# Four rounded and two raw weight slots, and a new order of half-units around the norms

## The reference, cut to what matters

```
for i in range(2):
    a = nsa_mixer(x, ...) if i == 0 else moba_mixer(x, ...)     # ends with  out @ w_o
    x = layer_norm(ALPHA * x + a, ln1_g[i], ln1_b[i])
    f = (silu(x @ wg) * (x @ wu)) @ wd                          # D_FF = 2816
    x = layer_norm(ALPHA * x + f, ln2_g[i], ln2_b[i])
```

## Time and profile before

| | us |
|---|---|
| median of 3 runs | 690.97 |
| lowest, highest | 690.02, 695.6 |
| profiled execution, its own time | 695.23 |
| its span in the trace | 693.5 |

### The profile page before, as it was taken

The page is one execution under the profiler, slowest core; times in us unless marked ns, Lnnn a source line. Parts: engine busy times, 40 slices in busy tenths (PEclk is TensorE's granted clock), DMA queues, the critical chain, the costliest instruction groups (busy, mean ns, idle before and its releaser), DMA issues.

```text
span 693.5 us, 8675 instructions
## 1 busy us (share of the span) xinstructions
PE 653.0 (94%) x3274; PEld 520.2 (75%) x3274; DVE 405.6 (58%) x529; ACT 309.2 (45%) x434; POOL 21.9 (3%) x64
## 2 busy tenths in 40 slices
PE   5899989998899999999997999989799999999995
PEld 4697865567688888888875888757578888888883
DVE  3645488875855544444458565675865444454446
ACT  4624557754253333444433544683343333444430
POOL 2000000000100000000002000000200000000001
PEclk9999999999999999999999999999999999999998
DMA  8954150002665554555543745303356555555501
GB/s 299 415 218 182 62 183 1 2 10 112 194 232 181 181 181 181 184 188 193 195 154 134 266 169 180 157 1 122 121 190 235 181 181 185 185 190 195 198 14 60
DMA packets 18282, 112.97 MB, mean 163 GB/s; under 512 B 2768, under 2 KB 3024, under 8 KB 5584
## 3 DMA queue, kind: packets, MB, share of 16 engines
q1 hardware_dynamic: 16384, 103.18, 41.3%
q10 hardware_dynamic: 720, 5.24, 2.0%
q0 software_dynamic: 1152, 4.19, 1.7%
HBM read 111.56 MB, written 1.05 MB: 162 GB/s over the span
## 4 chain that ended last, share of the span: by engine, by line
PE 76%; DVE 13%; ACT 4%; issue 2%; POOL 2%; SPq 1%; DMA 1%; POOLq 0%; DVEq 0%
PE ps L963 23%; PE ps L965 22%; PE ps L964 22%; DVE w_lo L640 3%; ACT arena L512 2%; DVE neg_max L790 1%; PE ps L1220 1%; DVE bn L856 1%; DVE x L851 1%; PE ps L1137 1%; DVE x L874 1%; DMA raw<-stream 1%; DVE arena L807 1%; PE ps L1068 1%; POOL rstd L367 1%
## 5 line engine op out<-in xcount | busy, mean ns | idle before, releaser
L640 DVE TENSOR_TENSOR w_lo<-raw,w_hi 128x2048 fp32r<-128x2048 f32 (+1 forms) x98 | 220.1, 2248 | 137.9 <-ACT w_hi L385 137.7
L963 PE MATMUL ps<-w_hi,a_hi 128*128 128x512 f32 x592 | 238.5, 403 | 16.3 <-DVE w_lo L640 11.4
L964 PE MATMUL ps<-w_lo,a_hi 128*128 128x512 f32 x592 | 233.5, 394 | 0.0
L965 PE MATMUL ps<-w_hi,a_lo 128*128 128x512 f32 x592 | 233.3, 394 | 0.0
L385 ACT ACTIVATE w_hi<-raw 128x2048 fp32r<-128x2048 f32 (+1 forms) x98 | 184.0, 1877 | 110.1 <-PE ps L965 103.4
L963 PEld LDWEIGHTS ps<-w_hi,a_hi 128*128 128x128 f32 x592 | 113.0, 191 | 43.4 <-DVE w_lo L640 12.3
L965 PEld LDWEIGHTS ps<-w_hi,a_lo 128*128 128x128 f32 x592 | 112.8, 191 | 24.5
L964 PEld LDWEIGHTS ps<-w_lo,a_hi 128*128 128x128 f32 x592 | 112.8, 191 | 22.2
L963 PE MATMUL ps<-w_hi,h_hi 128*128 128x512 f32 x160 | 62.4, 390 | 0.0
L965 PE MATMUL ps<-w_hi,h_lo 128*128 128x512 f32 x160 | 62.3, 389 | 0.0
L964 PE MATMUL ps<-w_lo,h_hi 128*128 128x512 f32 x160 | 62.2, 389 | 0.0
(11 more groups left out here) (144 smaller groups left out, 499.8 us busy)
## 6 DMA issues: line engine op xcount, KB each, us to landing
raw<-stream SPq DMA_DIRECT2D x94, 1024.0 KB, 4.8
gain<-norms POOLq DMA_DIRECT2D x8, 512.0 KB, 5.0
arena<-w ACTq DMA_DIRECT2D x4, 1024.0 KB, 8.1
raw<-stream SPq DMA_DIRECT2D x4, 512.0 KB, 8.5
twice<-x_cols SPq DMA_DIRECT2D x4, 256.0 KB, 7.3
x<-x_rows ACTq DMA_DIRECT2D x1, 1024.0 KB, 4.9
out<-x SPq DMA_DIRECT2D x4, 256.0 KB, 2.1
wg_raw<-w_gates SPq DMA_DIRECT2D x1, 192.0 KB, 9.7
```

Source lines behind the costliest of these rows:

```text
L640: return nc.vector.tensor_tensor(dst, a, b, ALU.subtract)
L963: nc.tensor.matmul(dst, hi, m_hi, start=start, stop=False)
L964: nc.tensor.matmul(dst, hi, m_lo, start=False, stop=False)
L965: return nc.tensor.matmul(dst, lo, m_hi, start=False, stop=stop)
```

## The change

- `w_hi` and `w_lo` get four slots, `raw` gets two. A load now waits for the remainder of the unit two before; a rounding for TensorE to be done with the unit four before. ScalarE and VectorE take units one place earlier in most of the written order.
- Output projection: the half-units in the last two jobs are now of half 0, so that right after the last job the last two units complete the sums of half 0; then come the four half-units of half 1, with `turn_x` of half 0 between the second and the third. In `attend` ScalarE and VectorE make the fourth output unit inside the last job, where it was made after it.
- Norm: VectorE adds eps itself; GpSimd only does the power. VectorE makes `a_lo` of half 0 and two units' remainders before the first quarter of half 1, a third remainder before its last quarter.
- First chunk: between half 0 and half 1 TensorE does the first unit of the next chunk for half 0, half of its tiles before and half after `turn_x` of half 1. In norms 0 and 2 it first waits for `var_ready` of half 1, since the bank was still read. In the projection of layer 1 the second chunk then lacks that half-unit.
- Network: chunk 1 gets other PSUM banks and is written out on ScalarE and VectorE too; the loop over chunks 2 to 9 holds four chunks a pass on all three engines. `turn_x` for norm 1 goes ahead of the last 6 matmuls.
- Other places in which only an index, a bank or a bound of `round_to` or `rest_to` follows from this are left out below.

```diff
 UNIT = 2048
-SLOTS = 3
+RAW = 2
+SLOTS = 4
...
 
-        SUM_BANK = [0, 4, 0, 4]
+        CHUNK_BANKS = ((3, 1), (0, 3))
+
+        AT_ONCE = 4
+
+        SUM_BANK = [(2, 3, 0, 1), (4, 5, 6, 7)] * 2
+
+        TURN_BANK = [(4, 5, 6, 7), (0, 1, 4, 5)] * 2
...
-                    sp.wait_ge(lo_ready, (t - 1) * SLOTS + s + 1)
-                    unit = stream[bass.ds(t * SLOTS + s, 1), :, :].rearrange("a p n -> (a p) n")
+            with sp.Fori(1, UNITS // RAW) as t:
+                for s in range(RAW):
+
+                    sp.wait_ge(lo_ready, (t - 1) * RAW + s + 1)
+                    unit = stream[bass.ds(t * RAW + s, 1), :, :].rearrange("a p n -> (a p) n")
                     sp.dma_start(raw[:, s, :], unit).then_inc(raw_in[s], 16)
...
             def roots(l):
                 for half in range(HALF):
                     gp.wait_ge(var_ready, 2 * l + half + 1)
-                    link(nc.gpsimd.tensor_scalar(var_eps[:, l, half:half + 1], mean_var[:, l, half, 1:2],
-                                                 1.0, EPS, ALU.mult, ALU.add))
                     nc.gpsimd.tensor_tensor(rstd[:, l, half:half + 1], var_eps[:, l, half:half + 1],
...
-            def round_unit(s, arrived, used):
-                act.wait_ge(raw_in[s], arrived)
-                if used is not None:
-                    act.wait_ge(w_used, used)
-                copy(w_hi[:, s, :], raw[:, s, :]).then_inc(hi_ready, 1)
+            def round_unit(u, later=0):
+
+                act.wait_ge(raw_in[u % RAW], later * (16 // RAW) + 16 * (u // RAW + 1))
+                if u >= SLOTS:
+                    act.wait_ge(w_used, later + (u - SLOTS + 1))
+                copy(w_hi[:, u % SLOTS, :], raw[:, u % RAW, :]).then_inc(hi_ready, 1)
...
                         outputs_hi(i - 2)
-                    if i == jobs - 2:
-                        round_to(u + 3)
+                    if i >= jobs - 2:
+                        round_to(u + 3 + i - (jobs - 2))
...
-                nc.scalar.activation(silu[:, 0, :], ps[:, 0, 0:FC], ACT.Silu).then_inc(first_silu, 1)
+                silu_half(0, CHUNK_BANKS[0][0]).then_inc(first_silu, 1)
                 act.wait_ge(w_used, u0 + 2)
-                nc.scalar.activation(silu[:, 1, :], ps[:, 1, 0:FC], ACT.Silu).then_inc(silu_ready, 1)
-                round_to(u0 + 4)
+                silu_half(1, CHUNK_BANKS[0][1]).then_inc(silu_ready, 1)
+                round_to(u0 + 5)
                 hidden_hi(0)
-                round_to(u0 + 5)
-                with act.Fori(1, NFC - 1) as c:
-                    round_in(c, 2)
-                    silu_of(c, 3 * c + (u0 + 1))
-                    round_in(c, 3)
-                    hidden_hi(c)
-                    round_in(c, 4)
-                units[0] = u0 + 3 * (NFC - 1) + 2
+                round_to(u0 + 7)
+                act.wait_ge(w_used, u0 + 4)
+                silu_half(0, CHUNK_BANKS[1][0])
+                silu_half(1, CHUNK_BANKS[1][1]).then_inc(silu_ready, 1)
+                round_to(u0 + 8)
+                hidden_hi(1)
+                round_to(u0 + 9)
+                with act.Fori(0, (NFC - 3) // AT_ONCE) as t:
+                    for j in range(AT_ONCE):
+                        c, at = AT_ONCE * t + (2 + j), u0 + 3 * (2 + j)
+                        round_unit(at + 3, 3 * AT_ONCE * t)
+                        silu_of(c, 3 * AT_ONCE * t + (at + 1))
+                        round_unit(at + 4, 3 * AT_ONCE * t)
+                        hidden_hi(c)
+                        round_unit(at + 5, 3 * AT_ONCE * t)
+                units[0] = u0 + 3 * (NFC - 1) + 3
                 c = NFC - 1
-                round_to(u0 + 3 * c + 3)
+                round_to(min(UNITS, u0 + 3 * c + 4))
                 silu_of(c, u0 + 3 * c + 1)
                 hidden_hi(c, last_hi)
                 round_to(min(UNITS, u0 + 3 * c + 5))
...
 
                     dve.wait_ge(v_step, quarter_statistics(half, 1))
-                    nc.vector.bn_aggr(mean_var[:, l, half, :], bn[:, :, :].rearrange("p a b -> p (a b)")).then_inc(var_ready, 1)
-                    dve.wait_ge(var_ready, 2 * l + half + 1)
+                    aggregated = step(nc.vector.bn_aggr(mean_var[:, l, half, :], bn[:, :, :].rearrange("p a b -> p (a b)")))
+                    dve.wait_ge(v_step, aggregated)
+                    nc.vector.tensor_scalar(var_eps[:, l, half:half + 1], mean_var[:, l, half, 1:2],
+                                            EPS, None, ALU.add).then_inc(var_ready, 1)
 
...
                 finish(0)
                 if l < 3:
                     rest_to(u + 1)
-                quarter_statistics(1, 0)
-                if l < 3:
                     columns_lo(0, 0)
                     columns_lo(0, 1)
                     rest_to(u + 2)
+                quarter_statistics(1, 0)
+                if l < 3:
+                    rest_to(u + 3)
                 last_quarter_statistics(1)
                 finish(1)
...
-                with dve.Fori(1, NFC - 1) as c:
-                    rest_in(c, 2)
-                    hidden(c)
-                    rest_in(c, 3)
-                    hidden_lo(c)
-                    rest_in(c, 4)
-                units[0] = u0 + 3 * (NFC - 1) + 2
+                rest_to(u0 + 7)
+                dve.wait_ge(silu_ready, c0 + 2)
+                hidden_half(0, CHUNK_BANKS[1][0])
+                hidden_half(1, CHUNK_BANKS[1][1]).then_inc(h_ready, 1)
+                rest_to(u0 + 8)
+                hidden_lo(1)
+                rest_to(u0 + 9)
+                with dve.Fori(0, (NFC - 3) // AT_ONCE) as t:
+                    for j in range(AT_ONCE):
+                        c, at = AT_ONCE * t + (2 + j), u0 + 3 * (2 + j)
+                        rest_of_unit(at + 3, 3 * AT_ONCE * t)
+                        hidden(c)
+                        rest_of_unit(at + 4, 3 * AT_ONCE * t)
+                        hidden_lo(c)
+                        rest_of_unit(at + 5, 3 * AT_ONCE * t)
+                units[0] = u0 + 3 * (NFC - 1) + 3
                 c = NFC - 1
-                rest_to(u0 + 3 * c + 3)
+                rest_to(min(UNITS, u0 + 3 * c + 4))
...
-            def first_chunk(u, ready, l):
+            def first_chunk(u, ready, l, banks, next_bank):
 
 
                 for half in range(HALF):
-                    if half == 1:
-                        turn_x(l, half)
                     for unit in range(2):
                         pe.wait_ge(a_lo_ready, ready + 2 * half + unit + 1)
                         pe.wait_ge(lo_ready, u + unit + 1)
-                        last = rows_by_weights(u + unit, unit, half, half)
+                        last = rows_by_weights(u + unit, unit, half, banks[half])
                         if half == 1:
                             last.then_inc(w_used, 1)
-                    if half == 0 and l % 2 == 0:
-                        last.then_inc(first_sums, 1)
+                    if half == 0:
+                        if l % 2 == 0:
+                            last.then_inc(first_sums, 1)
+                            pe.wait_ge(var_ready, 2 * l + 2)
+                        pe.wait_ge(lo_ready, u + 3)
+                        rows_by_weights(u + 2, 0, 0, next_bank, tiles=range(2))
+                        turn_x(l, 1)
+                        rows_by_weights(u + 2, 0, 0, next_bank, tiles=range(2, 4))
 
...
-                        rows_by_weights(u + c, 0, 1, 2 + c)
+                        rows_by_weights(u + c, 0, 0, SUM_BANK[0][c])
                     turn_probs(j0 + i)
...
 
 
-                for unit in range(2):
-                    rows_by_weights(u + unit, 0, 0, unit).then_inc(w_used, 1)
-                for half in range(HALF):
-                    for unit in range(2, 4):
-                        pe.wait_ge(lo_ready, u + unit + 1)
-                        pe.wait_ge(a_lo_ready, a0 + 8)
-                        if unit == 3 and half == 1:
-                            turn_x(l, 0)
-                        last = rows_by_weights(u + unit, 1, half, 2 * half + unit - 2)
-                        last.then_inc(sums_done if half == 0 else w_used, 1)
+                for unit in range(2, 4):
+                    pe.wait_ge(lo_ready, u + unit + 1)
+                    pe.wait_ge(a_lo_ready, a0 + 8)
+                    rows_by_weights(u + unit, 1, 0, SUM_BANK[l][unit - 2]).then_inc(sums_done, 1)
+                for unit in range(4):
+                    if unit == 2:
+                        turn_x(l, 0)
+                    rows_by_weights(u + unit, unit // 2, 1, SUM_BANK[l][2 + unit % 2]).then_inc(w_used, 1)
...
+                first_chunk(u0, ready, l, CHUNK_BANKS[0], CHUNK_BANKS[1][0])
+
                 pe.wait_ge(first_h, u0 // U_FF1 + 1)
-                rows_by_weights(u0 + 2, 0, 0, 0)
+                rows_by_weights(u0 + 2, 0, 1, CHUNK_BANKS[1][1]).then_inc(w_used, 1)
                 turn_hidden(0)
-                rows_by_weights(u0 + 2, 0, 1, 1).then_inc(w_used, 1)
```

(35 more changed lines are left out.)

59 lines of the change are left out of this document (23 added, 36 removed).

## The result

The changed kernel takes **689.06 us** (median of 19 runs, 685.34 to 693.17), the kernel before, run beside it on the same chip, 693.26 (19 runs). The ratio is **0.9944 [0.9925, 0.9963]**: 3.9 us less, with an interval of 2.6 to 5.2. The forecast was 5.8 less. The moves did what they were meant to, but their worth was put too high: three terms of the sum and the one for the clock did not come out. The profiled execution of after takes 689.16 us with a span of 687.4, against 695.2 and 693.5 before.

The account below looks back on a forecast made before the run. TensorE was taken as the bound, busy 653.0 of 693.5 us. Terms -2.9 -1.9 -2.2 -0.7 -0.5 gave -8.2 us against the profiled execution, 3.4 of it clock; for the median run -5.8, so 685.2 us, range 680.5 to 690.5.

Parts of the forecast that it names:

- The new wait after attention: TensorE's first product after attention waits for a_lo behind a w_lo on VectorE: +1.26 us in layer 0, +1.9 in layer 2.
- The stretch B to E: Norms 0 and 2, from the first product after attention (B) to the end of first-chunk half 1 (E): 33.95 us.
- Norm 1: Around the norm between network 0 and the projections: waits of 1.7 and 1.05 us, yet -1.9 us in all.
- the loops and the back edge: Feed-forward loops with two raw slots, four chunks a pass and one longer backward jump per network: cost 0.
- Rival 1: The loop's back edge stalls on an instruction fetch, up to 3.4 us an edge: 685 to 692 us, chance 15%.
- Rival 2: The two-slot raw ring becomes the bound in the loops, passes lengthen to 18.0 us: 706 us, chance 7%.
- the clock: Half clock behind norms 0 and 2 expected not to come, 1.7 us each: 3.4 of the 8.2 us.
- rival 3: Time moved, not saved: larger new waits, or a clock fall after attention's wait, +1.7 us each: 688 to 691, 20%.
- norm 2's -2.2: Layer 2, end of attention to the transposes of chunk 1: -2.2 us net, a half clock included.
- h of chunk 1: Hidden rows in each network's chunk 1 come late, at E+15.4, because ScalarE rounds two units before silu: 1.15 us wait.
- Start: Kernel start, where TensorE waits for unit 2's load: -0.7 us, between a gain of 1.4 and a loss of 0.6.
- Tail: Kernel end, two half norms with 0.24 us each of GpSimd work exchanged: -0.5 us.

Follow-up runs that it names:

- e5: The kernel before, unedited, profiled a second time: 690.40 us, span 688.7.
- e7: The kernel before with 8 and 5 useless matmuls put into two waits in layers 0 and 2: 690.52 us, ratio 0.9975 to before.
- e8: The changed kernel, unedited, profiled a second time: 689.06 us, span 687.3.
- e9: The changed kernel with 5 and 7 useless matmuls in the wait for a_lo after attention (layers 0 and 2): 686.88 us, ratio 0.9936 to before.
- e1: The changed kernel with silu and the product h of chunk 1 ahead of the seventh unit's rounding and remainder: 684.18 us, ratio 0.9905 to before.
- e2: The changed kernel with VectorE making the fourth output unit's remainder behind the last a_lo of attention: 686.69 us, ratio 0.9935 to before.
- e6: The changed kernel with silu ahead of the raw unit and the last a_lo of attention ahead of the fourth output unit's remainder: 684.87 us, ratio 0.9892 to before.
- e3: The changed kernel with the output projection's half-units back in the old order, half 1 inside attention: 696.80 us, ratio 1.0077 to before.
- e4: The changed kernel without the early half-unit between the halves of the first chunk, done behind half 1 instead: 696.37 us, ratio 1.0074 to before.

## Where the prediction was right, and why its sum was wrong

One measure serves for all kernels: from the last product of attention to the transposes of chunk 1, in layers 0 and 2, read from TensorE's order of time.

| Kernel | layer 0 | layer 2 |
|---|---|---|
| before, first profile | 53.68 | 53.66 |
| before, second profile (e5) | 52.05 | 52.04 |
| before, filled (e7) | 52.07 | 52.05 |
| after, first profile | 51.44 | 53.64 |
| after, second profile (e8) | 51.93 | 53.77 |
| after, filled (e9) | 51.35 | 51.90 |
| e1 | 49.75 | 50.44 |
| e2 | 50.82 | 51.49 |
| e6 | 49.63 | 49.52 |
| e3 | 55.89 | 56.12 |
| e4 | 54.38 | 56.54 |

For e1 and e6 it shows 0.3 to 0.7 us too much gain, since that much of the wait for h comes back a chunk later.

**Right: the waits.** The new wait after attention was forecast 1.26 and 1.9 us: 1.26 and 1.91. The wait before the first transposes: gone. For var_ready 1.1: 0.85. For x of half 1 0.7: 0.53. The stretch B to E, forecast 33.95, came out at 33.94 (155.87 to 189.81). Norm 1: waits 1.7 and 1.05 forecast, 1.56 and 0.67 found, and -1.9 us forecast, -2.1 found.

**Right: the loops and the back edge, 0.** Rival 1 is out: the pass behind the branch is 16.79 us long with no gap before it, and from inside the loop of network 2 to the last matmul both kernels take 140.47 us. The branch at 270.0 stands 3.4 us ahead of the pass that begins at 273.40, as before. The Trainium skill (Runtime: NRT & Kernel Launch, Instruction fetch mechanics) has a jump beyond its two-page window stall on a fetch. TensorE shows no stall here, though by the prediction's working the target lies 2.3 packets back. Nor does the trace show a fetch: between 261.5 and 355 us, from ahead of the branch to behind the loop, the DMA view of after lists no packet on queue q8, which has 21 in the whole execution, and a single one of 8 KB on the other instruction queue, q14. If q8 is TensorE's, as the prediction's count of packets takes it to be, nothing was fetched for this jump, and the lead had nothing to hide. It is the same around the second jump (566 to 656 us). Rival 2 is out too: the passes did not lengthen.

**Wrong: the clock, the step "of which 1.7 each is the half clock that I expect not to come".** It was 3.4 of the 8.2 us against the profiled execution, and fails twice. The reason given for it, "since the longest wait there is now 1.1 us", looks past the new wait of 1.9 us that the prediction itself puts in front. First, the half clock behind norms 0 and 2 comes in some executions of before only: its second profile has neither, and both stretches are 1.6 us shorter. Second, the new wait after attention has one of its own behind it in layer 2, in both profiles of after (470.9 and 470.6). That is rival 3, to which the prediction gave 20%. The 689.06 us measured lie in that rival's range. For before, e7 shows that the pauses bring the clock down: filled, they leave a higher mean clock (0.9883 against 0.9836) and a shorter time. For after, the pair of e9 and the first profile (53.64 to 51.90 us in layer 2) fits this, and e1's profile shows that it isn't so in every execution. So norm 2's -2.2 was 0.0 between the first profiles: 1.7 of the difference is that new half clock, 0.3 the longer wait for h.

**Wrong: three sizes.** h of chunk 1 was put at E+15.4 and came at E+15.97 in layer 0, because the seventh unit landed at E+11.0 (200.82) and not at E+10.4; the waits are 1.50 and 1.42 (1.97 and 1.53 in the second profile) instead of 1.15. Start: -0.7 was forecast because a lone load takes 4.8 us. Unit 2's load took 7.86 us from its issue at 11.72 (8.11 in the second profile), hardly less than the 8.55 before. Unit 3's load did stay back (issued at 18.18, 13.41 before), but unit 2's was not alone for that: the norm weights, the small tensors and the last half-unit, all issued before it, landed until 17.22, and the DMA engines were busy through the whole stretch (share 1.02 in 11.72 to 19.58, 1.06 before). TensorE's wait for it ends at 23.90 in after and at 24.05 in the second profile of before, so the load gave some -0.2. Tail: -0.5 forecast, -0.2 found (8.7 to 8.4).

The -1.6 us of the start between the first profiles is mostly chance, as far as eleven profiles tell. The same last product of attention 0 starts at 155.93, 154.36 and 154.32 us in the three profiles with the old slots (both of before, and e7) and anywhere from 152.86 to 157.04 in the eight with the new ones, whose code is the same up to the last jobs of attention; the means are 154.9 and 154.6. What differs is when the first product can start (8.1 to 9.2 us) and where the half clocks fall in the first 100 us.

**The sum again, apart from the clock.** From profiles without a half clock that costs in the stretch: norm 0 -0.6 (52.05 to 51.44; forecast, less the clock, -1.2), norm 2 -0.1 (52.04 to 51.90 in e9; forecast -0.5), norm 1 -2.1 (-1.9), start and tail -0.4 (-1.2). That is **-3.2 us** where the prediction had -4.8. It added 1.0 for the clock and came to -5.8; measured are -3.9, which leaves 0.7 for the clock. So of the 1.9 us that the forecast was too high, 1.6 are the sizes and 0.3 the clock. An estimate of the clock's part from the runs is larger: the mean granted clock is 0.984 in 52 runs of before and 0.9877 in 19 of after. One half clock takes 1.7 of 690 us, 0.0025, so after has 1.5 fewer; the scatter of 23 runs of before (5.8 us more for 0.01 of clock less) gives 1.4 us to each, 2.1 in all. With that the sum is -5.3, just past the interval's end at -5.2. So the two accounts do not agree on how much of the gain is clock, 0.7 or 2.1 us. Part of the difference may be the wait for h, which moves by 0.5 us between two profiles, or the start; it stays open. What holds in both is that the sizes were put too high.

The absolute time was off by another 2 us, because the runs of before beside after lie at 693.26, not at 690.97.

## What to carry to other kernels

Two profiles of the kernel before cost little and show which half-clock stretches come again. But two aren't enough to tie one to a wait (after has one at 471 us in both profiles, e1 has the same wait and none); the mean granted clock of a dozen runs with the wait filled, beside as many without, says more (e7). When work is moved to fill one wait, look at what else stood under the moved work, and price the new pause with the clock that may follow it. And with fewer staging buffers, walk each queue again: an item that waits for a later load must not stand ahead of one that TensorE asks for sooner (e1: one line moved on each of two engines, 1.9 us less waiting for h).

## What the hardware showed unexpectedly

- A half clock can cost little or nothing where waits follow. In the second profile of before it stood at 171.0 to 174.4 (11 starts), yet the stretch took 52.05 us, as the filled kernel did without it (52.07): the wait of 0.7 us for a_lo behind it was gone, and that for x shrank from 1.16 to 0.68. The Trainium skill (TensorE: Matmul & The Clock Gate, Terms) puts the penalty at the throttled time times one less the granted share. By that it would be 1.7 us; the trace agrees where no wait follows (53.68 against 52.05) and not here. A half clock of 6.8 us at 82.3 us cost 1.8 where that rule gives 3.4: from the product at 79.75 to the one at 100.18 it is 20.43 us, against 18.64 between the same two in the first profile of before, which has none there and waits 1.4 us longer at its end.
- Useless matmuls can make a kernel faster: 26 more products in four waits, 0.9975 [0.9953, 0.9998] of the time, and a mean granted clock of 0.9883 instead of 0.9836.
- The mean granted clock of a run explains most of its scatter. Runs of before lay from 686.98 to 694.65 us in one series, with a standard deviation of 2.35 us; at equal clock, by the line of 5.8 us for 0.01, it is 0.95.
